# First chunk of the first feed-forward block: smaller pieces of x and of the weights, on two queues, and another order of the steps

## What is computed

```
def rmsnorm(x, gain):
    y = xf * lax.rsqrt(jnp.mean(xf * xf, axis=-1, keepdims=True) + EPS)
    return (y * gain)

def swiglu(x, w_gate, w_up, w_down):
    return (jax.nn.silu(x @ w_gate) * (x @ w_up)) @ w_down

x = x + 0.5 * swiglu(rmsnorm(x, ffn1_norm[l]), ffn1_w_gate[l], ffn1_w_up[l], ffn1_w_down[l])
```

## Time and profile before

| | us |
|---|---|
| three runs, median (lowest to highest) | 1150.67 (1150.43 to 1150.97) |
| the profiled execution, its time | 1150.78 |
| its span, from the first to the last instruction | 1149.0 |
| TensorE busy in the span | 1140.2 |
| VectorE, ScalarE, GpSimd busy | 780.1, 638.3, 72.4 |
| mean rate of the DMA engines | 180 GB/s; 314 in the first fortieth of the span |

### The profile page before, as it was taken

The page is one execution under the profiler, slowest core; times in us unless marked ns, Lnnn a source line. Parts: engine busy times, 40 slices in busy tenths (PEclk is TensorE's granted clock), DMA queues, the critical chain, the costliest instruction groups (busy, mean ns, idle before and its releaser), DMA issues.

```text
span 1149.0 us, 16118 instructions
## 1 busy us (share of the span) xinstructions
PE 1140.2 (99%) x5963; PEld 963.0 (84%) x5963; DVE 780.1 (68%) x1072; ACT 638.3 (56%) x936; POOL 72.4 (6%) x81
## 2 busy tenths in 40 slices
PE   8999999999999999999999999999999999999998
PEld 7888888888778888888888888888887788888887
DVE  4856656778857676566677656668687495766655
ACT  6545545657773565455565545556576745655542
POOL 3200000220100000000040000002110000000000
PEclk9999999999999999999999999999999999999999
DMA  9965554544534665556567555536445445655520
GB/s 314 299 201 192 183 185 145 182 148 148 182 134 162 220 220 183 184 193 198 174 155 241 186 183 189 195 99 214 147 154 177 172 142 190 230 186 194 195 87 37
DMA packets 138364, 207.34 MB, mean 180 GB/s; under 512 B 6818, under 2 KB 99028, under 8 KB 138292
## 3 DMA queue, kind: packets, MB, share of 16 engines
q1 hardware_dynamic: 137444, 205.55, 54.2%
q0 software_dynamic: 752, 0.79, 0.8%
q10 hardware_dynamic: 96, 0.02, 0.0%
HBM read 205.29 MB, written 1.05 MB: 180 GB/s over the span
## 4 chain that ended last, share of the span: by engine, by line
PE 95%; DVE 2%; ACT 1%; DMA 1%; issue 0%; SPq 0%; DVEq 0%; ACTq 0%
PE bank L526 27%; PE bank L493 17%; PE bank L497 16%; PE bank L496 16%; PE bank L530 14%; PE bank L507 1%; DVE w_low L1104 1%; DMA raw<-in_ffn_w_up 1%; PE bank L722 1%; PE bank L692 1%; PE bank L708 1%; PE bank L707 1%; PE bank L739 1%; DVE probs L1278 0%; DVE oT_low L1115 0%
## 5 line engine op out<-in xcount | busy, mean ns | idle before, releaser
L1104 DVE TENSOR_TENSOR w_low<-raw,w_high 128x1024 fp32r<-128x1024 f32 x388 | 471.1, 1232 | 287.2 <-ACT w_high L860 287.0
L860 ACT ACTIVATE w_high<-raw 128x1024 fp32r<-128x1024 f32 x388 | 402.2, 1054 | 322.3 <-PE bank L493 112.6
L526 PE MATMUL bank<-xT,w_high 128*128 128x512 f32 x1392 | 340.2, 391 | 0.5 <-DVE xT L1122 0.2
L526 PEld LDWEIGHTS bank<-xT,w_high 128*128 128x128 f32 x1392 | 255.2, 188 | 50.7 <-DVE xT L1122 0.6
L530 PEld LDWEIGHTS bank<-xT,w_low 128*128 128x128 f32 x1408 | 180.9, 191 | 7.4 <-issue 0.6
L530 PE MATMUL bank<-xT,w_low 128*128 128x256 f32 x1408 | 185.1, 283 | 0.4 <-DVE w_low L1104 0.4
L493 PE MATMUL bank<-w_high,xT 128*128 128x512 f32 (+1 forms) x448 | 177.1, 395 | 0.1
L497 PE MATMUL bank<-w_low,xT 128*128 128x512 f32 (+1 forms) x448 | 171.6, 383 | 0.0
L496 PE MATMUL bank<-w_high,xT 128*128 128x512 f32 (+1 forms) x448 | 171.4, 383 | 0.0
L493 PE MATMUL bank<-w_high,oT_high 128*128 128x512 f32 x416 | 162.3, 390 | 0.0
L497 PE MATMUL bank<-w_low,oT_high 128*128 128x512 f32 x416 | 161.9, 389 | 0.0
(11 more groups left out here) (129 smaller groups left out, 750.7 us busy)
## 6 DMA issues: line engine op xcount, KB each, us to landing
raw<-in_w_in SPq DMA_DIRECT2D x92, 512.0 KB, 4.4
raw<-in_ffn_w_down SPq DMA_DIRECT2D x88, 512.0 KB, 4.2
raw<-in_ffn_w_gate SPq DMA_DIRECT2D x87, 512.0 KB, 4.0
raw<-in_ffn_w_up SPq DMA_DIRECT2D x87, 512.0 KB, 5.0
raw<-in_w_out SPq DMA_DIRECT2D x16, 512.0 KB, 4.5
raw<-in_w_branch_c SPq DMA_DIRECT2D x8, 512.0 KB, 4.1
raw<-in_w_branch_b SPq DMA_DIRECT2D x4, 512.0 KB, 6.7
raw<-in_w_branch_a SPq DMA_DIRECT2D x4, 512.0 KB, 4.9
```

Source lines behind the costliest of these rows:

```text
L526: return nc.tensor.matmul(bank[b0 + n][:, :], w_high[:, slot, column(k, n)], xT[:, k], start=k == 0, stop=k == KB - 1)
L860: act.activation(w_high[:, slot], raw[:, in_slot, (p % 2) * 1024:(p % 2) * 1024 + 1024], ACT.Copy).then_inc(sem["high_ready"], 1)
L1104: dve.tensor_tensor(w_low[:, slot], raw[:, FILL_SLOT[p // 2], (p % 2) * 1024:(p % 2) * 1024 + 1024], w_high[:, slot].bitcast(F32), ALU.sub ...
```

## The change

Constants: GpSimd clears `zero` first and says so (`zero_ready`), then makes the identity (`ident_ready`), then the masks. TensorE's products of zeros wait for `zero_ready` alone, and are nine before the gains' transposition and five after the first transposes.

Transfers: x comes in three pieces of columns (0 to 255, 256 to 511, 512 to 1023), all on SP. SP starts with x's first piece; the row of gains follows. The weights of pair 0 are issued by ScalarE, between the first and the second of its three rows of gains; those of pairs 1, 2 and 3 by SP, pair by pair (two DMAs of 256 KB each), with x's last piece between pairs 1 and 2.

ScalarE: the activation on zeros stands before the gains. Then two blocks of xT, the high part of pair 0 in two halves of 512 columns (`half_high` tells of the first), two blocks, high part 1, the squares of x's first 512 columns (into `first_sq`), high part 2, four blocks, high part 3, the squares of the other 512 columns, high part 4 (before the load of silu's table), the row's copy, high part 5, and on as before. GpSimd adds the two sums of squares. VectorE makes low blocks and low parts in turns of two blocks and one part.

TensorE: for layer 0, `cold_chunk` takes the place of the former order. Pair 0 has no product of 512 columns: eight of 256 with the high weights (four on the first half of the high part), four transposes, eight low parts, eight with `w_low`. Pairs 1 to 3 have all their wide products first, which wait for `high_ready` and not for `low_ready`, and then those with `w_low`. The last four blocks are turned after the wide products of pair 1, the row of scales after those of pair 3. The other first chunks keep their order (`first_chunk`).

The diff, cut to its core:

```diff
-SILU_AT, ROW_AT = 4, 2
-WARM_BEFORE, WARM_AFTER = 8, 6
+SILU_AT, ROW_AT, COLD_ROW_AT = 4, 2, 1
+X_PIECES = (slice(0, 256), slice(256, 512), slice(512, 1024))
+WARM_BEFORE, WARM_AFTER = 9, 5
...
+        def first_rows(engine, p, landed):
+            v = raw[:, FILL_SLOT[p // 2]].rearrange("p (k g c) -> p k g c", k=4, g=2)[:, p % 2 * 2:p % 2 * 2 + 2]
+            for g, w in enumerate((a["ffn1_w_gate"], a["ffn1_w_up"])):
+                engine.dma_start(v[:, :, g], w[0:1, p * 2 * P:(p + 1) * 2 * P, 0:FC].rearrange("o (k p) c -> p (o k) c", p=P)
+                                 ).then_inc(landed, 16)
...
+            load_x(0)
             sp.dma_start(gain_rows[48:50, :], a["diff_subln"]).then_inc(rows_loaded, 16)
-            def load_x(cols):
-                columns = slice(512 * cols, 512 * cols + 512)
-                for half in range(HALVES):
-                    sp.dma_start(x[:, half, columns], a["x"][0, half * P:half * P + P, columns]).then_inc(x_loaded[cols], 16)
-            def first_rows(k0, landed):
-                v = raw[:, FILL_SLOT[0]].rearrange("p (k g c) -> p k g c", k=4, g=2)
-                for g, w in enumerate((a["ffn1_w_gate"], a["ffn1_w_up"])):
-                    sp.dma_start(v[:, k0:k0 + 2, g], rows(w, 0, k0, 2, 0, FC)).then_inc(landed, 16)
-            load_x(0)
-            first_rows(0, first_landed)
             load_x(1)
-            first_rows(2, fill_landed[FILL_SLOT[0]])
+            first_rows(sp, 1, fill_landed[FILL_SLOT[0]])
+            load_x(2)
+            first_rows(sp, 2, first_landed[2])
+            first_rows(sp, 3, fill_landed[FILL_SLOT[1]])
...
+            pool.memset(zero[:, :].bitcast(F32), 0.0).then_inc(zero_ready, 1)
             pool.memset(ident[:, :], 0.0)
+            pool.drain()
+            pool.affine_select(out=ident[:, :], in_=ident[:, :], compare_op=ALU.not_equal, fill=1.0, base=0,
+                               pattern=[[-1, P]], channel_multiplier=1).then_inc(ident_ready, 1)
...
+            def cold_chunk():
+                b0 = inner_bank(1)
+                def turn(piece, group, parts):
+                    pe.wait_ge(x_loaded[piece], 16 * HALVES)
+                    turn_group(0, ST_FFN1, group, x, parts)
+                turn(0, 0, (0,))
+                warm(WARM_AFTER)
+                full, high_part, low_part = inner_parts(PAIR_SLOT[0], b0)
+                pe.wait_ge(sem["blocks_high"], 1)
+                pe.wait_ge(half_high, 1)
+                for n in range(4):
+                    high_part(0, n, w_high, True)
+                pe.wait_ge(sem["high_ready"], value("high_ready", 0, 1))
+                for n in range(4):
+                    high_part(1, n, w_high)
+                turn(1, 0, (1,))
+                pe.wait_ge(sem["blocks_low"], 1)
+                for k in range(2):
+                    for n in range(4):
+                        low_part(k, n)
+                pe.wait_ge(sem["low_ready"], value("low_ready", 0, 1))
+                for k in range(2):
+                    for n in range(4):
+                        last = high_part(k, n)
+                last.then_inc(sem["pair_used"], 1)
+                for p in range(1, 4):
+                    full, high_part, low_part = inner_parts(PAIR_SLOT[p], b0, False)
+                    pe.wait_ge(sem["blocks_low"], p + 1)
+                    pe.wait_ge(sem["high_ready"], value("high_ready", 0, p + 1))
+                    for n in range(4):
+                        for k in (2 * p, 2 * p + 1):
+                            full(k, n)
+                    if p == 1:
+                        turn(2, 1, (0, 1))
+                    if p == 3:
+                        turn_row(0, 1)
+                    pe.wait_ge(sem["low_ready"], value("low_ready", 0, p + 1))
+                    for n in range(4):
+                        for k in (2 * p, 2 * p + 1):
+                            last = high_part(k, n)
+                        if p == 3 and n == 1:
+                            last.then_inc(sem["gate_done"], 1)
+                    last.then_inc(sem["gate_up_done" if p == 3 else "pair_used"], 1)
...
-            pe.wait_ge(constants_ready, 1)
+            pe.wait_ge(zero_ready, 1)
             warm(WARM_BEFORE)
+            pe.wait_ge(ident_ready, 1)
...
+                if layer == 0 and p == 0:
+                    act.activation(w_high[:, slot, 0:512], raw[:, in_slot, 0:512], ACT.Copy).then_inc(half_high, 1)
+                    act.activation(w_high[:, slot, 512:1024], raw[:, in_slot, 512:1024], ACT.Copy).then_inc(sem["high_ready"], 1)
+                    return
...
+            def cold_start():
+                blocks_high(0, ST_FFN1, 0, G_FFN1, (0,))
+                high(0, 0)
+                blocks_high(0, ST_FFN1, 0, G_FFN1, (1,))
+                high(0, 1)
+                squares(first_sq, slice(0, 512), True)
+                high(0, 2)
+                blocks_high(0, ST_FFN1, 1, G_FFN1)
+                high(0, 3)
+                act.wait_ge(x_loaded[2], 16 * HALVES)
+                squares(norm_sq, slice(512, 1024), False).then_inc(sem["squares_ready"], 1)
...
+                cold = layer == 0 and before == 0
+                if cold:
+                    high(layer, first + 4)
...
+                            if i == 0 and j == 0 and n == (COLD_ROW_AT if cold else ROW_AT):
+                                copy_row(layer, 2 if before else 1)
                             if n == (ROW_AT if i == 0 and j == 0 else SILU_AT):
-                                if i == 0 and j == 0:
-                                    copy_row(layer, 2 if before else 1)
                                 copy_rest(layer, i * 2 + (before + 1 + j))
                                 silu_gate(layer, i * 2 + (before + 1 + j))
-                            high(layer, p + n, i * 12, i)
+                            if not (cold and i == 0 and j == 0 and n == 0):
+                                high(layer, p + n, i * 12, i)
...
+                if n == 0:
+                    first_rows(act, 0, first_landed[0])
...
-                    low(layer, 0)
-                    blocks_low(layer, ST_FFN1, 0, G_FFN1)
-                    low(layer, 1)
-                    low(layer, 2)
-                    blocks_low(layer, ST_FFN1, 1, G_FFN1)
-                    low(layer, 3)
+                    for p in range(4):
+                        blocks_low(layer, ST_FFN1, p // 2, G_FFN1, (p % 2,))
+                        low(layer, p)
```

114 lines of the change are left out of this document (57 added, 57 removed).

## The result

The changed kernel takes **1152.43 us** (median of 20 runs, 1151.25 to 1153.69). The kernel before takes 1150.53 on the same chips (20 runs, 1149.80 to 1151.38). The ratio is 1.0016, with a 95% interval of 1.0009 to 1.0022: slower by 1.9 us, where 0.5 us faster was forecast. The times of the changed kernel lie in three lots, near 1151.3, 1152.4 and 1153.4. The execution shown here is of the third: 1153.59 with a span of 1151.8, against 1150.78 and 1149.0 in the earlier trace rows.

What follows compares the result with a forecast made beforehand. TensorE bounds the kernel, so only its start counts. R (6.74 to 6.7) and 0.75 us give 0.8 with a fast clock, 0.2 with a late one; the middle, 0.5, from 1150.67 gives 1150.2 us, range 1148.4 to 1152.5.

Steps and rivals of the forecast that it cites:

- The frame: TensorE's start: only the first 30 us count, and the moment its unbroken stretch begins carries to the end one to one.
- R: The moment at which TensorE transposes the gains: 6.74 us before the change, forecast 6.7, called the largest unknown.
- equal turns: DMA queues at the start: ACT's 0.5 MB and x's first 0.5 MB get through together, giving 7.1 us.
- fast TensorE: TensorE at 2.4 GHz from R on: second chunk's third pair starts 0.8 us earlier.
- TensorE stays slow: Rival, chance 0.20: idle before R, the clock must be earned again; 1151.9 if up at 12 us, 1152.5 at 13 to 14.
- the norm's chain on GpSimd: First chunk: from last square to power's end 1.5 us, plus 0.3 for one more addition; scale ready at +14.1, before TensorE asks.
- The chain from R: Order of work in the first chunk: it ends at R + 16.0 instead of R + 17.4.
- the wait for low part 6: Second chunk, after two pairs: TensorE wants it at +21.6, VectorE has it at +22.2, a wait of 0.65 us.
- No wait in the second chunk: Rival, chance 0.07: low part 6 in time after all, 0.65 us more gained, 1149.5.
- The 1.4 us gained from R: First chunk: first real product at +2.2 instead of +3.6 after R; net of the second chunk's wait 0.75 us.
- Everything after has slack: After the second chunk's wait for low part 6: nothing later was expected to cost time.
- rows early: Rival, chance 0.18: rows of gains land early, R = 4.6 to 5.5, 1.3 to 2.3 us gained, about 1148.7.

Runs made afterwards that it cites:

- both repairs: Changed kernel with 14 zero products, high part 5 before the row's copy and VectorE's low part 4 after the norm's power: 1150.22 us, ratio 0.9998.

## Why the prediction was wrong

**The frame held, but for its length.** What is lost at the start reaches the end one to one (1.8 us by the second chunk, 2.4 by its end, 2.75 in the third; span +2.8). The start is 45 us long, though, not 30.

**R was close, in part by luck.** 6.7 forecast, 7.03 in the profiled execution, 6.75 to 7.11 in the others in which TensorE waited for rows left where the change put them (7.00 and 7.19 where it was still busy with zeros). The value of equal turns, 7.1, is nearer to 7.03. But the trace contradicts the way to either: q10 had 78.7% against 13.3% from 3 to 5 us, ACT's weights were there at 6.05, and it was the last row, 0.8 us behind them, that set R. In sum the second queue moved hardly more (306 GB/s from 3 to 7 us, 299 before); it reordered what moved. The Trainium skill, "DMA: Bandwidth & Descriptors", section "Issuing engines are not separate DMA queues", says that the DMAs of all issuing engines run on the same 16 DMA engines and interleave; in the sum the trace bears that out.

**The step that failed first is the clock.** (First in time; the larger share of the miss is in the sum with a fast TensorE, see below.) The text had both ends, 0.8 us gained with a fast TensorE and 0.2 with a clock that comes up at 9 us, and took the middle, 0.3 us for the clock. It had the right rival, *TensorE stays slow*, with 0.20, and a price for it: 1151.9, or 1152.5 at 13 to 14 us. Measured: 1152.43, with 2.06 us between R + 18.9 and R + 16.8 in the profiled executions (forecast: 2.0 more than with a fast TensorE) and 1.2 in the medians. The argument against it, that a gap of 1.8 us may not undo the work before, was a hope without a row. The earlier trace rows had one for it: the zero products of the kernel before ran at 1.2 GHz for all of 3.78 us, so nine products of 4 us could not be counted on to bring the clock up before the hole. With R at 6.7 in the forecast itself, the hole was certain, and the rival deserved far more than 0.20. That its price of 1152.5 lies so near to the median is luck: it was made of 0.8 us gained and some 2.6 lost to the clock, where the medians show 0.7 lost with a fast TensorE and 1.2 to the clock. What neither case had is that the moment varies: in the profiled executions the clock came up among the last of nine zero products (3.94 us for them), or not before the fourteenth had nearly ended (6.28 us for fourteen), and the lots of times go with it as far as they were profiled.

**The second is the norm's chain on GpSimd.** It was to take 1.8 us from the reading of the last square to the power's end. It took 3.1 (21.5 to 24.62). Of the excess of 1.3, 0.95 is the step of 1.14 beside a low part; the addition took 0.75 with its drain instead of 0.3, itself held up by low part 3; handing over was 0.1 shorter. It had 0.65 us of cover (+14.1 against +14.75), and even with a fast TensorE the scale was there only at +15.5. The cost of an engine's step was taken from a row in which the neighbour was idle; the change moved the low parts beside it. Low parts 3 and 4 stand in GpSimd's way only because the squares moved behind them. With low part 4 moved, the kernel takes 0.4 us less. Without the addition it takes only 0.16 less, since the addition too ended just behind a low part (22.43 against 22.37), and the next step is held up in its place.

**The order of work.** The chain from R was forecast as R + 16.0 for the second chunk; with a fast TensorE it was R + 16.8. First product +2.36 instead of +2.2, last pair's wide products +13.2 instead of +12.9, and 0.5 for the row's transposition. The wait of 0.7 before the third pair's wide products is there to the digit by the pace (the eight products from 17.73 take 0.95, to 18.68; the pair starts at 19.38). So is the wait for low part 6, forecast as 0.65 and measured as 0.55. *No wait in the second chunk* didn't happen. The 1.4 us gained from R are 0.6 in the kernel with 14 zero products (R + 17.4 against R + 16.8) and 1.0 with both repairs.

**"Everything after has slack" was wrong by 0.3 us.** The low parts that come late in the second chunk make VectorE's sums on the third chunk's banks late. The prediction had only asked whether TensorE was idle there before, not how near VectorE was to making it so. VectorE was busy without a break from 28 to 34 us, a low part took 2.52 us at 36.88 beside `gates`, and the second sum on the banks ended at 41.43, 0.2 us before the fifth product of TensorE's row (40.74) would need it. Being late by 0.4 us more than TensorE was enough. With low part 6 in time TensorE's row takes 2.03 us, with the norm's scale in time as well 1.84, and the low part beside `gates` 2.78 and 2.54 us: both the late low part and the late work of GpSimd have a share in it.

**The rival *rows early* had the wrong price.** It let the chain move with R, by up to 2.3 us. Moved ahead (R = 5.12), the rows were followed by a wait for pair 0, and the first product came at 8.34, not at 7.3 (R + 2.2). The condition that the text names under what would make it wrong, "pair 0 later than it", is the one that holds there.

**The chances.** The text sums 0.10 for times above 1153.0, but its range ends at 1152.5; the 0.5 us between stand in no sum.

Added up from the medians: +0.7 with a fast TensorE (0.8 for low part 6 and the third chunk, 0.4 for GpSimd, together 1.0, less 0.3 that the new order gains), and +1.2 for the clock, make +1.9. Against the forecast that is a miss of 2.4 us: 0.9 for the clock (1.2 instead of 0.3), and 1.5 for the sum with a fast TensorE (0.8 us faster forecast, 0.7 slower measured). The profiled executions place most of the 1.5: the chain from R longer by 0.8 (0.5 of it the row's transposition), and 0.4 in the third chunk, where nothing was reckoned.

## What to carry to other kernels

Before work is moved so that an engine idles at the start, ask what that hole does to TensorE's clock, and fill it up to the moment at which data really come: five zero products were worth 1.2 us here, more than the whole reordering. Ask too whether the clock is up when the hole begins; near the moment at which it comes up, that differs from execution to execution. A step of GpSimd has two prices, beside an idle VectorE and beside one that reads two tiles; take the one that holds in the new order. An early order of DMAs is set by the smallest thing that everybody waits for: 24 KB of gains ahead of 512 KB of weights gave 2.0 us here, 1.2 of them through the clock.
